# Attention's keys and first queries turned and split in the front's last units

## The chip, the cores and the metric

One core of one Trainium2 chip runs the whole kernel. The metric is device time in microseconds (us) of that core; a result is the median of several runs.

## What is computed

One layer of a hybrid backbone over 1024 latent tokens and 256 context tokens, width 1024, in fp32. What matters here is its first half:

```python
hc = _rms(ctx, norm1) * (1 + cc1) + ch1
kvc = hc @ w_in[:, OFF_K:OFF_G]                  # context keys and values
kc = _rms(kvc[..., :KV_W] per head, k_norm)
hx = _rms(x, norm1) * (1 + sc1) + sh1
zx = hx @ w_in                                   # 3 x 512 Hyena, 512 q, 128 k, 128 v, 2 x 1024 gates
q = _rope(_rms(q per head, q_norm), cos, sin)    # 8 heads of 64
k = _rope(_rms(k per head, k_norm), cos, sin)    # 2 heads of 64
y_b = _window_attention(q, k, v, kc, vc, sink)   # own block of 128 and its neighbours, all 256 context keys
```

`_window_attention` takes the softmax over the scores of at most 384 near keys (masked to a distance of 128), the 256 context keys and a sink logit. Then come the Hyena convolution, the merge of both branches, and 16 routed experts.

## The kernel before, in words

The kernel is a row of blocks, with a barrier of all engines between them: `front` (about 0 to 453 us), `attention` (to 619 us), then `spectra`, `convolve`, `merge`, `experts`. In each block every engine has its own instruction list, written out by hand, and semaphores order them. An engine runs its list in order: a wait holds all that stands behind it.

**Front.** Tokens are normed, modulated, turned and split into two parts, `h_hi` and `h_lo` (a rounded fp32r part and the rest), each 128 x 8 x 1280: eight slices of the width by 1280 token columns, the last 256 of them context. `w_in` is loaded in 17 units of 256 columns and split the same way by ScalarE (`high_part`) and VectorE (`weights_low`). TensorE (`project`, in the order of the list `groups`) makes each product of three fp32r matmuls (`three`, L220). Units 0 to 2 give q, k, v, written to `qkv` token by token; units 3 to 8 the Hyena inputs; units 9 to 16 the gates. `GATES` is 9, and from unit 3 on a unit is four groups (two halves of the columns by two halves of the tokens). ScalarE evicts each group from one of six banks. `first[u]` is the index of unit u's first group. A unit of gates is 96 matmuls of 512 columns on TensorE, some 22 us.

VectorE's list runs unit by unit, in this order: the low part of the next unit's weights; in units 9 and up, that unit's parts of the remaining modulation (`ada_part`, L620: two in each of units 9 to 11, one in unit 12, none later); then the norming and rotation of one token tile's heads (`norm_heads`, L647), from unit 4 to unit 13, ten tiles, the eight latent ones first and then the two of the context; in units 3 to 8 the short convolution. A part of the modulation waits for the load of its weights, which SyncE issues only when the part before is done (L389), and for the column sums that TensorE makes at the end of a unit (`column_sums`, L752) for the parts before it. VectorE signals each normed tile with the semaphore `qn_ready`. In unit 15 it makes the gate rows with a matmul of TensorE through the bank `p_rows` (L787).

**Attention** works in blocks of 128 queries (n = 0 to 7) by 8 heads, 64 steps u. Before the steps: TensorE turns the context's and the first two tiles' keys (`turn_k`, job NEAR) and the first queries (`turn_q`), ScalarE writes their high parts, VectorE their low parts and zeros, ScalarE copies the high part to the other half of the partitions (`k_beside`), four fills keep TensorE at work (`fill`, L1160: matmuls whose result nobody reads), and GpSimd makes three mask tables. Only then come the first scores (L1173). The keys of tiles 2 to 5 (MID) are handled at step 1, those of 6 and 7 (FAR) at step 3, and the next queries at step 4 of block 0 and step 1 of later blocks. A step is: scores of step u+2 (L1182 to L1189) once the exp of step u has freed their half of `p_s`; on VectorE the maximum and the shift of u+2 (L1071, L1073); exp on ScalarE (L1032); turning of the probabilities (L1197, L1203); their copies to `pT` by VectorE (L1083) and ScalarE (L1012). At steps 2 to 6 of a block the products with the values of the block before (L1223).

Keys stand in `kS` and `k_lo` (128 x 2 x 1280) with context first, so a block's near keys are one run of up to 384 columns.

Of the kernel before, what the change touches and what calls it, by code (L numbers as in the profile page):

```python
# [20 lines left out]
P = 128  # L21
D = 1024
L = 1024
# [110 lines left out]
def build(nc, A, out):  # L134
    root = ExitStack()
    with root:
# [37 lines left out]
        with ExitStack() as s12:  # L174
# [3 lines left out]
            with ExitStack() as s:  # L178
                sbh, _ = scope(s)

                with ExitStack() as below:
                    g["ada"] = scope(below)[0]("ada", [P, 2 * D // 512, KD, 512])
                g["h_hi"] = sbh("h_hi", [P, KD, LA], F32R)
                g["h_lo"] = sbh("h_lo", [P, KD, LA], F32R)
                front(g)
            g["tf"] = right.enter_context(nc.sbuf_tensor("dft_in", [P, 10, FC, LQ], F32, side="right"))
            g["decay"] = filters.enter_context(nc.sbuf_tensor("decay_in", [P, NT, HY], F32, side="right"))
            g["fpm"] = filters.enter_context(nc.sbuf_tensor("fpm", [H2, ORD, 2, HY], F32, side="right"))
            g["y_out"] = filters.enter_context(nc.sbuf_tensor("y_out", [P, 2, 512], F32, side="right"))
            g["y_stored"] = [nc.alloc_semaphore(name=f"y_stored{i}") for i in range(2)]  # L190
            attention(g)
# [35 lines left out]
def front(g):  # L227
# [30 lines left out]
    with ExitStack() as s:  # L258
# [7 lines left out]
        with ExitStack() as below:  # L266
# [3 lines left out]
            ub = sbb("ub", [P, L + 2])  # L270
# [4 lines left out]
            wrow = sbb("wrow", [P, NG, HD])  # L275
            cos, sin = sbb("cos", [P, NT, ROT]), sbb("sin", [P, NT, ROT])
            xn = sbb("xn", [P, NG, HD])
        x = sb("x_in", [P, NTA, D])
        hf = sb("hf", [P, 3, 512])
        rows1, rows2 = sb("rows1", [80, P]), sb("rows2", [56, P])  # L280
        junk = sb("junk", [P, D])[:]
# [40 lines left out]
        q_root, q_step, rope_step, qn_ready = sem("q_root_ready"), sem("q_step"), sem("rope_step"), sem("qn_ready")  # L322
        padded, conv_step, z_ready = sem("padded"), sem("conv_step"), sem("z_ready")
# [5 lines left out]
        ROWS_AT = UNITS - 2  # L329

# [5 lines left out]
        with nc.Block() as block:  # L336
            @block.sync
            def _(sp):
# [40 lines left out]
                sp.wait_ge(lo_ready, len(GROUPS))  # L379
                for u in range(UNITS):  # L380
                    if u == 2:
                        sp.wait_ge(sin_ready, 3)
# [23 lines left out]
            def _(pool):  # L406
# [6 lines left out]
                pool.memset(spare[0:H2, 6144:6144 + 2 * H2], 0.0).then_inc(f_zero, 1)  # L413

            @block.scalar
            def _(act):
# [19 lines left out]
                def evacuate(i):  # L436
# [10 lines left out]
                    else:  # L447
# [6 lines left out]
                        if h == 1:  # L454
                            act.wait_ge(evacuated, i + 1)
                            act.dma_start(g["gate_dram"][P * n:P * n + P, :], gs[:, n % 2, :])\
                               .then_inc(g_stored[n % 2], 16)

# [46 lines left out]
                act.wait_ge(padded, 1)  # L505
                for i in range(EARLY, len(groups)):
# [10 lines left out]
                    evacuate(i)  # L517

            @block.vector
            def _(dve):  # L520
# [126 lines left out]
                def norm_heads(i):  # L647


                    nonlocal rope_steps  # L650
                    x = qkv[:, i, 0:NG * HD].rearrange("p (h d) -> p h d", d=HD)
                    r_ = rstd[:, i, :].unsqueeze(2).broadcast_to([P, NG, HD])
                    if i:
                        dve.wait_ge(qn_ready, i)
# [14 lines left out]
                    dve.wait_ge(z_ready, min(2 * (i + 1), NZ))  # L669
# [33 lines left out]
                dve.memset(ub[:], 0.0).then_inc(padded, 1)  # L703
                dve.memset(ssq[:], 1.0).then_inc(ssq_ready, 1)
                dve.wait_ge(ssq_ready, 1)
                for u in range(UNITS):
# [7 lines left out]
                    if u == ROWS_AT:  # L714
                        gate_rows()
# [35 lines left out]
            def _(pe):  # L751
# [6 lines left out]

                def project(i):
# [19 lines left out]
                    if u >= 2 and i == last[u] - 1:  # L779
                        for m in (ada_parts(0) if u == 2 else []) + ada_parts(u - 1):  # L780
                            column_sums(m)
                    q = i - first[ROWS_AT] - 1
                    if 0 <= q < 4:
                        pe.wait_ge(diag_ready, q + 1)
                        if q:
# [80 lines left out]
def attention(g):  # L866
# [11 lines left out]
    with ExitStack() as s:  # L878
        sb, ps = g["scope"](s)
        nsink = sb("nsink", [P, NKV, GRP])  # L880
# [1571 lines left out]
```

## Time and profile before

| | us |
|---|---|
| median of 3 runs | 2245.38 |
| lowest, highest run | 2242.11, 2246.43 |
| span of the profiled execution | 2242.3 (its own time isn't listed) |
| front, start to last TensorE group | 452.4 |
| attention, to the first work of the next block | 453.8 to 619.7 |
| TensorE busy | 2145.9 |
| VectorE, ScalarE busy | 1655.7, 1147.0 |

A timeline row gives an instruction's start and duration, its engine (PE is TensorE, PEld its weight loads, DVE VectorE, ACT ScalarE, POOL GpSimd, SP SyncE), its line, what it writes and reads, and in brackets how long its engine was idle before it and who ended that. PEclk is TensorE's granted clock as a share of 2.4 GHz; it has two levels, 1.2 and 2.4 GHz, so a mean between 0.5 and 1 is a mix of both. A matmul's duration is longer than the spacing of a stream of them.

### The profile page before, as it was taken

How to read it: one execution, taken by the hardware profiler on the slowest of the kernel's cores; microseconds unless marked ns; L12 is line 12 of the kernel's file. 1: busy time of each engine (PE TensorE's matmuls, PEld its weight loads, DVE VectorE, ACT ScalarE, POOL GpSimd, SP SyncE). 2: the span in 40 equal slices, each digit the busy share in tenths (PEclk: the TensorE clock that was granted, in tenths of full speed). 3: DMA queues.
4: the chain of work that ended last, by engine and by line, in shares of the span. 5: the costliest groups of instructions: out<-in, count | busy, mean ns of one | idle time of the engine just before them, and what ended most of it. 6: DMA issues, size and time to landing. Idle time of an engine off the chain costs nothing.

```text
span 2242.3 us, 27253 instructions
## 1 busy us (share of the span) xinstructions
PE 2145.9 (96%) x10057; PEld 1695.6 (76%) x10057; DVE 1655.7 (74%) x1707; ACT 1147.0 (51%) x1201; POOL 175.8 (8%) x53
## 2 busy tenths in 40 slices
PE   7999999989999999999489999999999999999998
PEld 2998888856567776468468888888888888888886
DVE  3668754167654897553688889889889989898986
ACT  3521212165500220121257777777777777777775
POOL 0000000010000000000011011111011111011100
PEclk9999999999999999999789999999999999999999
DMA  8134454130020232643569999999999999999993
GB/s 305 61 98 163 142 178 141 47 118 13 17 80 6 70 131 91 221 168 113 197 236 364 393 394 380 380 378 380 399 391 380 378 382 384 396 387 380 380 378 121
DMA packets 183291, 539.38 MB, mean 241 GB/s; under 512 B 15231, under 2 KB 57355, under 8 KB 182708
## 3 DMA queue, kind: packets, MB, share of 16 engines
q1 hardware_dynamic: 172768, 506.72, 60.3%
q0 software_dynamic: 4752, 16.78, 2.9%
q10 hardware_dynamic: 5700, 14.90, 1.7%
q8 instruction: 48, 0.79, 0.1%
q14 instruction: 23, 0.19, 0.0%
HBM read 502.71 MB, written 35.65 MB: 240 GB/s over the span
## 4 chain that ended last, share of the span: by engine, by line
PE 49%; DVE 2%; DMA 0%; issue 0%; ACT 0%; POOL 0%; POOLq 0%
PE p_y L222 5%; PE p_y L224 5%; PE p_a L222 5%; PE p_a L224 5%; PE p_y L223 5%; PE p_a L223 5%; PE p_b L224 5%; PE p_b L223 5%; PE p_b L222 5%; PE p_t L2350 1%; PE p_t L2341 1%; DVE idx_rows L2305 1%; DVE late L2308 0%; DVE vals L2303 0%; DMA g1row<-xn_dram,idx_e 0%
## 5 line engine op out<-in xcount | busy, mean ns | idle before, releaser
L2246 DVE TENSOR_TENSOR r_lo<-ring,r_hi 128x2048 fp32r<-128x2048 f32 x384 | 865.8, 2287 | 62.8 <-ACT r_hi L2205 56.0
L2205 ACT ACTIVATE r_hi<-ring 128x2048 fp32r<-128x2048 f32 x384 | 731.0, 1915 | 154.4 <-PE p_b L224 74.7
L222 PE MATMUL p_y<-r_hi,a_hi 128*128 128x512 f32 x512 | 205.3, 401 | 0.0
L222 PE MATMUL p_a<-r_hi,x_hi 128*128 128x512 f32 x512 | 202.5, 396 | 1.0 <-DVE x_lo L2257 1.0
L224 PE MATMUL p_y<-r_hi,a_lo 128*128 128x512 f32 x512 | 200.0, 391 | 0.0
L224 PE MATMUL p_a<-r_hi,x_lo 128*128 128x512 f32 x512 | 199.8, 390 | 0.0
L223 PE MATMUL p_a<-r_lo,x_hi 128*128 128x512 f32 x512 | 199.2, 389 | 0.0
L223 PE MATMUL p_y<-r_lo,a_hi 128*128 128x512 f32 x512 | 199.2, 389 | 0.0
L222 PE MATMUL p_b<-r_hi,x_hi 128*128 128x512 f32 x512 | 199.2, 389 | 0.0
L223 PE MATMUL p_b<-r_lo,x_hi 128*128 128x512 f32 x512 | 199.2, 389 | 0.0
L224 PE MATMUL p_b<-r_hi,x_lo 128*128 128x512 f32 x512 | 199.2, 389 | 0.0
L222 PE MATMUL p_z<-h_hi,w_hi 128*128 128x512 f32 x448 | 177.0, 395 | 0.0
L224 PE MATMUL p_z<-h_hi,w_lo 128*128 128x512 f32 x448 | 174.5, 390 | 0.0
L223 PE MATMUL p_z<-h_lo,w_hi 128*128 128x512 f32 x448 | 174.4, 389 | 0.0
L2168 POOL DMA_INDIRECT g1row<-xn_dram,idx_e x16 | 121.4, 7587 | 58.5 <-issue 43.3
L2174 POOL DMA_INDIRECT out_x<-late,idx_s x17 | 45.3, 2666 | 914.6 <-DVE late L2296 914.6
L224 PEld LDWEIGHTS p_y<-r_hi,a_lo 128*128 128x128 f32 x512 | 96.1, 188 | 21.0
L224 PEld LDWEIGHTS p_a<-r_hi,x_lo 128*128 128x128 f32 x512 | 96.1, 188 | 20.5
L222 PEld LDWEIGHTS p_a<-r_hi,x_hi 128*128 128x128 f32 x512 | 96.2, 188 | 20.2 <-issue 1.4
L223 PEld LDWEIGHTS p_b<-r_lo,x_hi 128*128 128x128 f32 x512 | 96.1, 188 | 20.0
L222 PEld LDWEIGHTS p_b<-r_hi,x_hi 128*128 128x128 f32 x512 | 96.1, 188 | 20.0
L224 PEld LDWEIGHTS p_b<-r_hi,x_lo 128*128 128x128 f32 x512 | 96.1, 188 | 19.9
(319 smaller groups left out, 3577.7 us busy)
## 6 DMA issues: line engine op xcount, KB each, us to landing
ring<-in_w_gate SPq DMA_DIRECT2D x128, 1024.0 KB, 8.4
ring<-in_w_up SPq DMA_DIRECT2D x128, 1024.0 KB, 8.5
ring<-in_w_down SPq DMA_DIRECT2D x128, 1024.0 KB, 12.0
w_raw<-in_w_in SPq DMA_DIRECT2D x17, 1024.0 KB, 6.1
ada_rest<-in_ada_w SPq DMA_DIRECT2D x16, 1024.0 KB, 5.3
ada<-in_ada_w SPq DMA_DIRECT2D x8, 1024.0 KB, 15.3
gate_dram<-zs ACTq DMA_DIRECT2D x16, 512.0 KB, 2.6
x_normed<-gate_dram SPq DMA_DIRECT2D x16, 512.0 KB, 4.3
```

Of the source, the lines that this page charges most:

```text
L222: pe.matmul(out, a_hi, b_hi, start=start, stop=False)
L223: pe.matmul(out, a_hi, b_lo, start=False, stop=False)
L224: return pe.matmul(out, a_lo, b_hi, start=False, stop=stop)
L2168: pool.indirect_dma_start(out=xe[:], out_offset=None, in_=g["xn2_dram"][:, :], in_offset=bass.IndirectOffsetOnAxis(ap=idx_e[:, 0:1], axis=0))\
L2174: pool.indirect_dma_start(out=rows, in_=part, in_offset=None, out_offset=bass.IndirectOffsetOnAxis(ap=idx_s[:, at:at + 1], axis=0), comput ...
L2205: act.activation(r_hi[:, i % PARTS], ring[:, i % RAW], ACT.Copy).then_inc(hi_ready, 1)
L2246: dve.tensor_tensor(r_lo[:, i % PARTS], ring[:, i % RAW], r_hi[:, i % PARTS].bitcast(F32), ALU.subtract).then_inc(lo_ready, 1)
L2305: dve.max_index(rows[:, at], vals[:, at], aff).then_inc(found, 1)
L2341: mm = pe.transpose(p_t[:, bank, P * k:P * k + P], xe[:, P * (4 * q + k):P * (4 * q + k) + P], ident[:])
L2350: mm = pe.transpose(p_t[:, q % 2, P * k:P * k + P], au[:, q % 2, P * k:P * k + P], ident[:])
```

## The change

- The keys of all tiles and the queries of block 0 are turned and split in the front. TensorE does it through the bank `p_rows`, after the second group of unit 9 (NEAR), the second of unit 12 (MID), and the first (FAR) and third (queries) of unit 14. It waits for `qn_ready` of 4, 8, 10, 10. ScalarE and VectorE make the parts with the same instructions as before; the one new split is that NEAR's context and token parts go to two places, so its low part is four instructions of 256 columns.
- `norm_heads` takes the context tiles first (`HEAD_ORDER`), in units 4 and 5, and the latent tiles in units 6 to 13. So the eighth is tile 5, in unit 11.
- The latent keys' parts go into the columns of `h_hi` and `h_lo` that held the normed context tokens (columns 1024 to 1279 of each slice), 128 per key head: slice c holds the keys of tile c. A block's near keys are now up to three runs of 128 columns, 1280 columns apart. The context's keys have a buffer of their own.
- Queries of later blocks and probabilities take the places of the normed latent tokens.
- Masks and the sink table are made in the front; the front's buffers have other places, and the scratch `junk` lies in `ub`, of which now only the two edge columns are cleared.
- Attention begins with its scores. After the first two steps' scores come two fills (four before) and a wait for the table `sel`. The queries of block 1 are turned at step 1 of block 0.

The diff, cut to its core:

```diff
@@ front @@
+        HEAD_ORDER = list(range(NT, NTA)) + list(range(NT))
+        NEAR, MID, FAR, FIRST_Q = range(4)
+        KEY_TILES = ((NT, NT + 1, 0, 1), (2, 3, 4, 5), (6, 7))
+        TURNED_AT = {first[GATES] + 1: NEAR, first[GATES + 3] + 1: MID, first[GATES + 5]: FAR, first[GATES + 5] + 2: FIRST_Q}
+        NORMED = {NEAR: 4, MID: 8, FAR: NTA, FIRST_Q: NTA}
+        LOW_AT = {GATES + 1: (NEAR,), GATES + 4: (MID,), GATES + 5: (FAR, FIRST_Q)}
...
+            token = tile[rows, :, L + P * kv:L + P * kv + P]
+            beside = g["k_context"][rows, int(tile is h_lo), kv, :].rearrange("p (c t) -> p c t", t=P)
...
+                def turned_high(job):
+                    act.wait_ge(turned, job + 1)
...
+                    if job == NEAR:
+                        act.wait_ge(z_ready, NZ)
...
                     evacuate(i)
+                    if i in TURNED_AT:
+                        turned_high(TURNED_AT[i])
...
-                def norm_heads(i):
+                def norm_heads(p):
+                    i = HEAD_ORDER[p]
...
+                    if u == GATES:
+                        zero_beside()
...
                     if QKV_UNITS < u <= QKV_UNITS + NTA:
                         norm_heads(u - QKV_UNITS - 1)
+                    for job in LOW_AT.get(u, ()):
+                        turned_low(job)
...
+                def turn_early(job):
+                    pe.wait_ge(qn_ready, NORMED[job])
+                    if job == NEAR:
+                        pe.wait_ge(sin_ready, 3)
+                    else:
+                        pe.wait_ge(part_lo, job)
+                    if job == FIRST_Q:
+                        for j in range(GRP):
+                            mm = pe.transpose(p_rows[:, P * j:P * j + P], qkv[:, 0, P * j:P * j + P], ident[:])
+                    else:
+                        for n, t in enumerate(KEY_TILES[job]):
+                            mm = pe.transpose(p_rows[:, P * n:P * n + P], qkv[:, t, HD * NH:HD * NG], ident[:])
+                    mm.then_inc(turned, 1)
...
                             column_sums(m)
+                    if i in TURNED_AT:
+                        turn_early(TURNED_AT[i])
@@ attention @@
-                turn_k(K_NEAR, p_q)
-                turn_q(0, p_o)
-                fill(4)
-                pe.wait_ge(masks, 3)
-                pe.wait_ge(k_zero, NKV)
...
-                    pe.matmul(out[:, a:512], both, kS[:, kv, keys], start=True, stop=False)
-                    pe.matmul(out[:, a:512], both, k_lo[:, kv, keys], start=False, stop=False)
+                    pe.matmul(near, both, keys(h_hi, kv, n), start=True, stop=False)
+                    pe.matmul(near, both, keys(h_lo, kv, n), start=False, stop=False)
...
                 scores(0)
                 scores(1)
-                pe.wait_ge(qk_lo, 2)
-                turn_k(K_MID, p_q)
-                turn_k(K_FAR, p_o)
+                fill(2)
+                pe.wait_ge(small_in, 16)
...
-                    if h == turn_at(n) and n + 1 < NT:
-                        pe.wait_ge(qk_lo, q_job(n + 1) - 1)
+                    if h == 1 and n + 1 < NT:
+                        if n:
+                            pe.wait_ge(qk_lo, n)
```

## Rows read from the trace of the kernel before

**Rows 1.** The page, busy time of the engines: us, share of the span, instructions.
```profile
PE 2145.9 (96%) x10057; PEld 1695.6 (76%) x10057; DVE 1655.7 (74%) x1707; ACT 1147.0 (51%) x1201; POOL 175.8 (8%) x53
```

**Rows 2.** Table by stretches, 100 to 450 us: length, then engines' busy us.
```profile
sum 350.00, PE 350.00 PEld 295.65 DVE 191.00 ACT 67.18 POOL 0.00; mean PE 87.50 PEld 73.91 DVE 47.75 ACT 16.80 POOL 0.00
```

**Rows 3.** Timeline of attention, weight loads of four transposes: start, duration, instruction.
```profile
471.62 0.47 PEld L1152 LDWEIGHTS p_turned<-ident,qkv 128*128 128x128 f32 x4
```

**Rows 4.** Timeline, VectorE alone, gate units 10 and 11; in brackets idle before, releaser.
```profile
315.40 0.35 DVE L626 TENSOR_SCALAR ada_acc<-ada_rest,sil 128x256 f32<-128x256 f32 x1 [11.43 <-PE p_mod L755]
...
333.18 2.28 DVE L531 TENSOR_TENSOR w_lo<-w_raw,w_hi 128x2048 fp32r<-128x2048 f32 x1
338.08 0.35 DVE L626 TENSOR_SCALAR ada_acc<-ada_rest,sil 128x256 f32<-128x256 f32 x1 [2.61 <-PE p_mod L755]
...
347.37 0.35 DVE L626 TENSOR_SCALAR ada_acc<-ada_rest,sil 128x256 f32<-128x256 f32 x1 [5.29 <-DMA ada_rest<-in_ada_w]
...
355.21 0.49 DVE L678 TENSOR_TENSOR qkv<-work 128x320 f32<-128x320 f32 x1
```

**Rows 5.** Timeline, TensorE alone, end of unit 11 and unit 12.
```profile
337.46 0.95 PE L755 MATMUL p_mod<-ones,ada_acc 128*128 128x1 f32 x8
338.28 0.48 PE L222 MATMUL p_z<-h_hi,w_hi 128*128 128x512 f32 x1
...
349.26 0.39 PE L222 MATMUL p_z<-h_hi,w_hi 128*128 128x512 f32 x1
```

**Rows 6.** Timeline, all engines, from attention's start to its first scores.
```profile
453.81 1.81 DVE L1116 TENSOR_SCALAR k_lo<-ones 64x1280 fp32r<-64x1280 f32 x2 [17.09 <-PEq L336]
453.81 0.63 PE L1157 MATMUL p_turned<-ident,qkv 128*128 128x128 f32 x4 [1.45 <-PEq L336]
...
454.71 3.60 PE L1163 MATMUL p_context<-qkv,ident 128*128 128x512 f32 x8
...
458.07 1.28 ACT L1032 ACT_TABLE_LOAD   x1
...
458.77 0.35 PE L1182 MATMUL p_s<-kS,qS 128*128 128x256 f32 x1 [0.46 <-DVE qS L1054]
```

**Rows 7.** Timeline, all engines, attention's first block of queries.
```profile
461.52 0.39 PE L1182 MATMUL p_s<-kS,qS 128*128 128x256 f32 x1 [0.66 <-ACT probs L1032]
...
463.15 1.18 ACT L992 ACTIVATE kS<-p_turned 64x512 fp32r<-64x512 f32 x2
...
465.65 0.69 ACT L1032 ACTIVATE probs<-p_s,nm 128x512 f32<-128x512 f32 x1
...
466.49 0.39 PE L1182 MATMUL p_s<-kS,qS 128*128 128x256 f32 x1 [2.01 <-ACT probs L1032]
...
469.76 0.69 ACT L1032 ACTIVATE probs<-p_s,nm 128x512 f32<-128x512 f32 x1
...
474.27 1.39 DVE L1054 TENSOR_TENSOR qS<-p_turned,qS 64x512 fp32r<-64x512 f32 x2
...
475.72 0.60 PE L1182 MATMUL p_s<-kS,qS 128*128 128x384 f32 x1 [2.18 <-DVE qS L1054]
```

**Rows 8.** TensorE's timeline at 51 us; then stretches: us, busy, granted clock, DMA.
```profile
51.06 0.35 PE L222 MATMUL p_z<-w_hi,h_hi 128*128 128x256 f32 x1 [3.09 <-DVE w_lo L531]
...
52.00:56.00 4.00, 4.00 (x24) 4.00 (x23) 3.90 (x7) 1.83 (x4) 0.00 (x0) 0.57 0.87 263
...
476.00:480.00 4.00, 3.99 (x21) 3.14 (x20) 1.86 (x5) 1.37 (x4) 0.00 (x0) 0.59 0.00 0
...
728.00:735.00 7.00, 6.31 (x20) 4.88 (x21) 0.00 (x0) 2.04 (x4) 0.00 (x0) 0.53 0.97 309
```

**Rows 9.** Groups by line and form, 450 to 620 us: busy us, mean ns.
```profile
L1182 PE MATMUL p_s<-kS,qS 128*128 128x384 f32 x48 | 21.4, 445 | 2.4 <-DVE qS L1054 2.2 <-ACT probs L1032 0.3
...
L1152 PEld LDWEIGHTS p_turned<-ident,qkv 128*128 128x128 f32 x28 | 3.3, 141 | 0.0
```

**Rows 10.** One line's instructions, L1544: ns least, median, most; first and last start.
```profile
L1544 PEld LDWEIGHTS p_j<-ident,ya x64: 195/212/231, 726.4 to 831.2; 128*128 128x128 f32 x64
```

More of the change, by code:

```diff
@@ L188, in build @@
[L188 to L191, printed above, removed]
+                g["masks"] = [sbh(n, [P, P], BF16) for n in ("negI", "m_prev", "m_next")]
+                g["nsink"], g["sinks"] = sbh("nsink", [P, NKV, GRP]), sbh("sinks", [P, GRP, NKV])
@@ new lines, in build @@
+                with ExitStack() as below:
+                    sbw, _ = scope(below)
+                    g["wrow"] = sbw("wrow", [P, NG, HD])
+                    g["cos"], g["sin"] = sbw("cos", [P, NT, ROT]), sbw("sin", [P, NT, ROT])
+                    g["xn"] = sbw("xn", [P, NG, HD])
+                sbh("head_space", [P, 1792])
+                front(g)
+                g["tf"] = right.enter_context(nc.sbuf_tensor("dft_in", [P, 10, FC, LQ], F32, side="right"))
+                g["decay"] = filters.enter_context(nc.sbuf_tensor("decay_in", [P, NT, HY], F32, side="right"))
@@ L192, in build @@
+                g["fpm"] = filters.enter_context(nc.sbuf_tensor("fpm", [H2, ORD, 2, HY], F32, side="right"))
+                g["y_out"] = filters.enter_context(nc.sbuf_tensor("y_out", [P, 2, 512], F32, side="right"))
+                g["y_stored"] = [nc.alloc_semaphore(name=f"y_stored{i}") for i in range(2)]
+                attention(g)
             give_back()
@@ L889, in attention @@
         r_t = sb("r_t", [NH, 2, P])
-        probs = sb("probs", [P, 3, 640])
-        pT = sb("pT", [P, 2, NKV, 5, GRP, P])
+        probs = parts[:, 1, KD - 3:KD, 0:640]
+        pT = [[parts[:, b, 0:5, 512 * kv:512 * kv + 512].rearrange("p c (j t) -> p c j t", j=GRP) for kv in range(NKV)]
+              for b in range(2)]
         o_raw = sb("o_raw", [P, 512])
@@ L918, in rows, with keys, context @@
             return slice(HD * kv, HD * kv + HD)
-        NEAR_JOB, MID_JOB, FAR_JOB = 1, 3, 4
-        KEYS = {NEAR_JOB: (0, 512), MID_JOB: (512, 1024), FAR_JOB: (1024, LA)}
-        KEYS_AT = {1: MID_JOB, 3: FAR_JOB}
+        def keys(table, kv, n):
+            b = blocks(n)
+            return table[:, b[0]:b[-1] + 1, L + P * kv:L + P * kv + P]
+        def context(side, kv):
+            return g["k_context"][:, side, kv, :]
         def values_bank(n):
             return p_w if n == NT - 1 else p_o
-        def turn_at(n):
-            return 1 if n else 4
-        def q_job(n):
-            return n + 4 if n else 2
         with nc.Block() as block:
@@ L1130, in _ @@
                     window_copy(u)
[L1131 to L1133 removed]
+                    if h == 2 and n + 1 < NT:
                         q_low(n + 1, p_q)
@@ L1153, in turn_q @@
                     mm.then_inc(qk_turned, 1)
-                def turn_k(tiles, bank):
-                    for i, t in enumerate(tiles):
-                        mm = pe.transpose(bank[:, P * i:P * i + P], qkv[:, t, HD * NH:HD * NG], ident[:])
-                    mm.then_inc(qk_turned, 1)
                 def fill(count):
@@ L1187, in scores @@
                         pe.matmul(out[:, 512 - P:512], negI[:], m_next[:], start=False, stop=True)
-                    pe.matmul(out[:, 512:768], both, kS[:, kv, 0:LC], start=True, stop=False)
-                    pe.matmul(out[:, 512:768], both, k_lo[:, kv, 0:LC], start=False, stop=True).then_inc(s_done, 1)
+                    pe.matmul(out[:, 512:768], both, context(0, kv), start=True, stop=False)
+                    pe.matmul(out[:, 512:768], both, context(1, kv), start=False, stop=True).then_inc(s_done, 1)
                 def turn_probs(u):
```

213 lines of the change are left out of this document (118 added, 95 removed).

## The prediction

> **What bounds the kernel now.** I read three things in turn. The page first: TensorE is busy for 96% of the span, and the places where it isn't are few [rows 1]. Then a table by stretches over the front: from 100 to 450 us TensorE is busy in every microsecond, VectorE in 191 of the 350 and ScalarE in 67 [rows 2]. So in the front each microsecond in which TensorE waits, or transposes, is a microsecond of the kernel. Then the timelines, at the two places that the change touches: gate units 11 and 12 of the front, and the first 25 us of attention. Barriers stand between front, attention and what follows, and nothing that the change touches crosses them but loads that land long before their use, so a shift at either place reaches the end whole.
>
> **The front: what is added.** Fourteen transposes move into TensorE's stream: 4 for the near keys, 4, 2 and 4. Four of them take 0.47 us of weight loads, which set their pace, in attention [rows 3]: 14 x 0.118 = 1.6 us, and with an estimated 0.1 us for each of four switches 2.0 us. I find no cover: 1.6 to 2.4.
>
> **The front: a new wait.** The middle keys are turned after the second group of unit 12, and TensorE waits there until eight tiles are normed. The new order puts the context tiles first, so tile 5 is the eighth, at the place where tile 7 stands now: VectorE's work of unit 11, behind that unit's two parts of the modulation. That place is tied to TensorE and to a load: part 13 waits for the column sums at the end of TensorE's unit 11 (337.46) and starts at 338.08; part 14 waits 5.29 us for its load, which is issued only when part 13 is done; the norming follows, and its last write ends at 355.21 + 0.49 = 355.70 [rows 4, 5]. TensorE starts unit 12 at 338.28 and is through its second group at 349.26, where the third group's first matmul starts now [rows 5]. It would wait 355.70 - 349.26 = 6.4 us. Behind it stand all further projections; VectorE's next parts and ScalarE's evictions wait for TensorE and move with it, so nothing makes up for it. Whether VectorE can be there sooner or later: the moved zeroing (1.81 us [rows 6], unit 9) and the near keys' low part (four halves of 256 columns, estimated at 1.7 us from 1.39 for two of 512 [rows 7], unit 10) lie ahead of it. The zeroing goes into a wait of 11.43 us at 315.40; the low part delays the low weights of unit 12 from 333.18 + 2.28 to 337.2, with TensorE wanting them at 338.28, so it costs nothing, with about 1 us to spare [rows 4]. The other three turnings have their tiles and parts in time: the near ones need the fourth norming, from unit 7; the last tile is normed in unit 13, with one part of the modulation in unit 12 and none in 13, some 10 us before unit 14's first group ends.
>
> A wait of this length lowers the clock behind it. After 3.09 us without TensorE work the clock is at its lower level, 1.2 GHz, for most of 52 to 56 us (mean 0.57); later in the kernel it stays there from 728 to 735 us (0.53) [rows 8]. In a stream without gaps I take the first, 3.4 us at half speed: 1.7 us, with 0 and 3.5 as ends. The Trainium skill (TensorE: Matmul & The Clock Gate, HAM oscillation) says that a long wait between matmul bursts makes the next burst start slow; by that rule too the wait costs more than its length, and the trace agrees.
>
> Small things. The masks go to the front's start, where GpSimd has nothing else; they were ready ahead of the queries' low part, so nothing is gained by it. On SyncE one small load goes ahead of the norm weights, and VectorE waits for it before the low weights of unit 2, where it has time. The padding's clearing shrinks, and only ScalarE waited for it. In all these the cover is TensorE's unbroken stream [rows 2], so 0 for each; if the small load came late, VectorE's slack there would have to be used up first. **Front: 2.0 + 6.4 + 1.7 = 10.1 us more** (8.0 to 12.3).
>
> **Attention's start: what goes.** Now the first scores start at 458.77, after the keys and queries were turned, copied and split, and the third scores at 461.52 [rows 6, 7]. Changed, TensorE starts scores as its first work at 453.81: 4.96 us sooner. Then two fills stand in its queue, of 0.9 us each (eight matmuls in 3.60) [rows 6]: 1.2 + 1.8 = 3.0 us from first to third scores, where they are now 2.75 apart. So the third scores come 4.7 us sooner. The new wait there for the selection table costs nothing if its load (issued at about 453.8) lands by 456.8; the trace shows only that two such loads had landed before the scores at 458.77, so up to 1.9 us could be lost. VectorE and ScalarE have nothing ahead of the first maximum and the first exp; the activation table load of 1.28 us, now at 458.07 [rows 6], then starts at 453.8 and ends before the first exp at about 455.7. The Trainium skill (ScalarE: Activation LUTs, What ACT_TABLE_LOAD costs) adds a drain of 1.38 us to each load; by that figure the estimate is an exp 0.8 us later, and the third scores about 0.5 us later. No row here separates a drain from idle time, and the sum leaves it out.
>
> **The first block of queries.** From the third to the ninth scores it now takes 461.52 to 475.72 = 14.2 us [rows 7]. In it ScalarE splits the middle keys (463.15 to 465.65), so that the third exp, whose bank the fifth scores wait for, starts at 465.65 instead of about 463.4: the fifth scores come at 466.49 instead of 464.3, 2.2 us. The far keys hold the fifth exp until 469.76 and cost 1.1 us in the same way. The next queries are turned at the block's fifth unit, and their low part (474.27 + 1.39) holds the ninth scores until 475.72 instead of about 473.4: 2.3 us [rows 7]. These 5.6 us go. In return the next queries are turned at the second unit: 1.2 us of ScalarE and 1.39 of VectorE, half of what the middle keys took of ScalarE; I take half their loss, 1.1 (0.4 to 2.2). Gain 4.5 us (3.0 to 5.2). With it goes the idleness ahead of 475.72, behind which the clock is 0.59 for 4 us [rows 8]: up to 1.7 us, I take 1.2, for TensorE still waits a little here. Later blocks issue the same instructions on other addresses. **Attention: 4.7 + 4.5 + 1.2 = 10.4 us less** (11.6 = 4.7 + 5.2 + 1.7; at the least 5.8, with the load's 1.9 lost, 3.0 for the block and nothing for the clock).
>
> **The sum** is -0.3 us. The three runs shown have a median of 2245.38; the profiled execution's span is 2242.3, near the lowest of them (2242.11), and its own time isn't listed. On the median: 2245.1. I call changes within 0.2% (4.5 us, about what can be told from none) no change; this comes out so because the new wait pays back what attention's start gains.
>
> **Rivals.**
> A: the wait in unit 12 doesn't come, because the eighth norming is done earlier than I read. For it: VectorE is idle for nearly half of these units [rows 2]. Against: the idleness is waiting for TensorE and a load [rows 4]. Then front +2.0, attention -10.4: 2237.0, faster. 0.15.
> B: it is slower, by the keys' new layout. The near keys are read in up to three runs of 128 columns, 1280 apart, by 128 matmuls. The first of each 384-column pair takes 445 ns as a contiguous read [rows 9]; no row shows such a read. The nearest are transposes of every fourth element, whose weight loads take 212 ns [rows 10] against 141 for contiguous ones [rows 9], though that is a step at each element and here it is one in 128. At 71 ns each: 9.1 us, and with the forecast's -0.3 2254.2. It decides from 35 ns each (4.5 us). 0.06.
> C: the wait comes and the low clock behind it lasts 7 us, as at 728, while the first block keeps part of its losses and its low clock: front 12.3, attention 7.5: 2250.2. 0.12.
> D: the wait comes without a low clock and attention gives its most: 8.4 - 11.6: 2242.2. 0.17.
> Forecast: 0.5.
>
> **Numbers.** 2245.1, range 2237 to 2251: from A to C, which leaves B and the far ends out. Faster by over 0.2% is A with some of D's tail: 0.19. Slower is B and the half of C and its tail: 0.15. Within: 0.66.
>
> **What would show it.** TensorE idle for about 6 us behind the second group of unit 12, ended by VectorE's last rotation write, then 3 to 4 us of matmuls at 1.2 GHz; four short bursts of transposes; the front's last matmul some 10 us later; first scores right at attention's start, third scores 3.0 us behind; ninth about 13 behind the first; no clock below 1 at the second block. I am wrong if the transposes of the middle keys follow their group without a gap, or if near-key matmuls are longer than before.

## The result, and the profile after

| | before | changed |
|---|---|---|
| median of 5 runs, us | 2245.45 | 2253.72 |
| lowest, highest | 2242.11, 2246.86 | 2252.21, 2255.94 |
| span of the profiled execution | 2242.3 | 2251.7 |

The ratio is 1.0039, with a 95% interval of 1.0026 to 1.0051: slower by 8.3 us, outside the predicted range of 2237 to 2251.

Both halves of the prediction, front and attention, can be looked up. The new wait comes first, in the timeline of TensorE alone, units 11 and 12, changed kernel (start, duration, instruction, idle before it and who ended it):

```profile
344.14 0.95 PE L873 MATMUL p_mod<-ones,ada_acc 128*128 128x1 f32 x8
...
362.81 1.11 PE L888 MATMUL p_rows<-ident,qkv 128*128 128x128 f32 x4 [6.37 <-DVE qkv L761]
363.58 0.77 PE L241 MATMUL p_z<-h_hi,w_hi 128*128 128x512 f32 x1
...
365.44 0.50 PE L242 MATMUL p_z<-h_lo,w_hi 128*128 128x512 f32 x1
365.77 0.39 PE L243 MATMUL p_z<-h_hi,w_lo 128*128 128x512 f32 x1
```

And VectorE alone, which ends it:

```profile
339.97 0.42 DVE L797 TENSOR_TENSOR h_lo<-p_rows,h_hi 64x256 fp32r<-64x256 f32 x1
340.42 2.29 DVE L613 TENSOR_TENSOR w_lo<-w_raw,w_hi 128x2048 fp32r<-128x2048 f32 x1
344.75 0.35 DVE L708 TENSOR_SCALAR ada_acc<-ada_rest,sil 128x256 f32<-128x256 f32 x1 [2.04 <-PE p_mod L873]
...
354.44 0.35 DVE L708 TENSOR_SCALAR ada_acc<-ada_rest,sil 128x256 f32<-128x256 f32 x1 [5.69 <-DMA ada_rest<-in_ada_w]
...
362.27 0.48 DVE L761 TENSOR_TENSOR qkv<-work 128x320 f32<-128x320 f32 x1
362.68 2.28 DVE L613 TENSOR_TENSOR w_lo<-w_raw,w_hi 128x2048 fp32r<-128x2048 f32 x1
```

These rows answer to [rows 4, 5]: VectorE does the same work in the same order, with the near keys' low part (`h_lo`, 339.97) put ahead of it. The wait was forecast at 6.4 us and is 6.37. The clock behind it, in the table by stretches (length, busy us of PE, PEld, DVE, ACT, POOL with counts, granted clock, DMA):

```profile
356.00:360.00 4.00, 0.44 (x2) 0.00 (x1) 3.82 (x8) 0.60 (x1) 0.00 (x0) 0.85 0.49 162
360.00:362.80 2.80, 0.00 (x0) 0.00 (x0) 2.73 (x8) 0.00 (x0) 0.00 (x0) 0.50 0.99 340
362.80:364.00 1.20, 1.19 (x5) 1.19 (x6) 1.20 (x1) 0.03 (x1) 0.00 (x0) 0.50 0.10 32
364.00:366.00 2.00, 2.00 (x6) 1.53 (x6) 0.96 (x1) 1.94 (x4) 0.00 (x0) 0.59 0.00 0
366.00:368.00 2.00, 2.00 (x10) 1.63 (x9) 0.00 (x0) 0.47 (x1) 0.00 (x0) 1.00 0.92 235
```

TensorE is granted 1.2 GHz from about 358.8, inside the wait, until about 365.6 (0.59 over the two us from 364). What lies between 362.81 and 365.77, four transposes and five matmuls of 512 columns, takes 2.96 us; at the full clock it would be 0.47 + 5 x 0.234 = 1.64 (0.234 is the spacing of this kernel's stream at the full clock). So the low clock costs 1.3 us by this sum (forecast 1.7), and 1.4 by run 4 below.

Attention, TensorE alone, again the changed kernel:

```profile
470.95 0.40 PE L243 MATMUL p_z<-h_hi,w_lo 128*128 128x512 f32 x1
472.83 0.36 PE L1242 MATMUL p_s<-h_hi,q_first 128*128 128x256 f32 x1 [1.48 <-PEq L374]
...
475.61 0.49 PE L1242 MATMUL p_s<-h_hi,q_first 128*128 128x256 f32 x1
...
485.74 0.41 PE L1242 MATMUL p_s<-h_hi 128*128 128x384 f32 x1
...
489.34 0.45 PE L1242 MATMUL p_s<-h_hi 128*128 128x384 f32 x1 [0.37 <-ACT h_parts L1126]
```

These rows answer to [rows 6, 7]. The third scores come 2.78 us behind attention's start (7.71 before, so 4.93 sooner; forecast 4.7), the ninth 10.13 us behind the third (14.20 before; 4.07 gained, forecast 4.5). Attention now ends 156.4 us after its first scores at 472.83 (next block's first matmul at 629.26, L1408), where it took 619.76 - 453.81 = 165.95: **9.5 us less**, against 10.4 forecast.

But the front's last matmul starts at 470.95, and before it was at 451.97: **19.0 us later**, not 10.1. That is the miss, and the page of the profile shows where to look. Section 5 of the changed kernel's page has the same matmul form in the experts (`p_b`) and in the front (`p_z`); the mean ns of one is the last number before the second bar:

```profile
L241 PE MATMUL p_b<-r_hi,x_hi 128*128 128x512 f32 x512 | 199.2, 389 | 0.0
...
L241 PE MATMUL p_z<-h_hi,w_hi 128*128 128x512 f32 x448 | 181.0, 404 | 0.0
L243 PE MATMUL p_z<-h_hi,w_lo 128*128 128x512 f32 x448 | 177.8, 397 | 0.0
L242 PE MATMUL p_z<-h_lo,w_hi 128*128 128x512 f32 x448 | 177.8, 397 | 0.0
```

And the same group in the kernel before, its page:

```profile
L222 PE MATMUL p_z<-h_hi,w_hi 128*128 128x512 f32 x448 | 177.0, 395 | 0.0
L224 PE MATMUL p_z<-h_hi,w_lo 128*128 128x512 f32 x448 | 174.5, 390 | 0.0
L223 PE MATMUL p_z<-h_lo,w_hi 128*128 128x512 f32 x448 | 174.4, 389 | 0.0
```

The front's projections of units 3 to 16, whose instructions the change leaves alone, are longer by 7 to 9 ns each, from the first one of unit 3 on. The starts say it more sharply. Take the time from one matmul's start to the start of the third after it, a sum of three spacings: it is 680 ns before, in every unit, and 702 to 703 now. 1344 matmuls / 3 x 21.5 ns = 9.6 us. That is an estimate from spacings; runs 4 and 10 below, which differ in the weights' place alone, put their last projection at 463.16 and 454.00 and so make it 9.2 us. With the wait 6.4, the clock 1.4 and the transposes 2.0 (run 10) that is the whole of the 19.0.

No wait explains it: the idle column says 0.0. What the change did do to this stream is in the layout. In units 3 to 16 the weights are the loaded (stationary) operand and the tokens the moving one. `h_hi` and `h_lo` stand where they stood, at bytes 57472 and 98432 of each partition. The four weight tiles stood at byte 157824 and, one behind the other, 8192 further each; in the changed kernel `w_hi0` begins at 169952. The slices that the matmuls take out of these tiles start multiples of 256 bytes into them, so a tile's start modulo 256 holds for every slice.

### The profile page after: what moved, and what is told of

Read it like the earlier page. It is cut to its first block, busy times and chain, and to the rows that moved or that the text cites. A ratio compares the mean times of both kernels' runs of the same rounds, so it can differ in the third digit from the quotient of the medians.

```text
span 2251.7 us, 27262 instructions
## 1 busy us (share of the span) xinstructions
PE 2152.8 (96%) x10053; PEld 1695.6 (75%) x10053; DVE 1654.9 (73%) x1712; ACT 1147.9 (51%) x1205; POOL 174.8 (8%) x53
## 4 chain that ended last, share of the span: by engine, by line
PE 49%; DVE 2%; DMA 0%; issue 0%; ACT 0%; POOL 0%; POOLq 0%
PE p_y L241 5%; PE p_a L241 5%; PE p_y L243 5%; PE p_a L243 5%; PE p_y L242 5%; PE p_a L242 5%; PE p_b L241 5%; PE p_b L242 5%; PE p_b L243 5%; PE p_t L2406 1%; PE p_t L2397 1%; DVE idx_rows L2361 1%; DVE late L2364 0%; DVE vals L2359 0%; DMA g1row<-xn_dram,idx_e 0%
## 6 DMA issues: line engine op xcount, KB each, us to landing
ada<-in_ada_w SPq DMA_DIRECT2D x8, 1024.0 KB, 15.3
```

## The experiments

"Tokens" are `h_hi` and `h_lo`, "weights" the four tiles `w_hi0`, `w_lo0`, `w_hi1`, `w_lo1`; numbers 0 and 1 serve even and odd units. "Three spacings" is the sum above, the median of the 84 such sums inside the four groups of a unit, worked out from the starts in the trace. A ratio is to the kernel before, run beside it.

**1. Weights moved in the kernel before** (`e1`).

```diff
-        w_hi, w_lo = [sb("w_hi0", [P, KD, UW], F32R)], [sb("w_lo0", [P, KD, UW], F32R)]
+        def shifted(t, at):
+            return t[:, at:at + KD * UW].rearrange("p (k n) -> p k n", k=KD)
+        AT = (8, 8, 8, 8)
+        w_hi = [shifted(sb("w_hi0", [P, KD * UW + 16], F32R), AT[0])]
+        w_lo = [shifted(sb("w_lo0", [P, KD * UW + 16], F32R), AT[1])]
...
```

> The kernel before, with one thing changed: each of the four tiles of split weights is 64 bytes longer and its weights start 32 bytes into it, so that they start at an address that is 32 modulo 64, as in the changed kernel, instead of 0 modulo 64. Nothing of the change itself is in it. Theory (place of the stationary operand): the front's matmuls of 512 columns, whose stationary operand is a weight tile, follow each other at 0.234 us instead of 0.227, a group of 24 takes 5.62 instead of 5.44 us, and the 56 such groups of units 3 to 16 bring about 10 us: about 2255, 1.0045 of before. Rival 1 (the spacing comes from what VectorE, ScalarE or the loads do at the same time in the changed kernel, in their new places or order): spacing stays 0.227 and the time 2245. Rival 2 (the moving operand, the tokens, which did not move, must lie at a certain distance from the weights): some other spacing, the same in even and odd units only by chance.

Measured: 2249.47 (10 runs), ratio 1.0023 (1.0013 to 1.0032), three spacings 693 in odd units, 695 to 696 in even ones, and 700 in unit 3, although it has the same tiles as the other odd units. So moving the weights alone, in a kernel without the change, slows the stream: rival 1 falls. But 693 isn't 703, and the time rose by half of what was expected: the start modulo 64 isn't the whole of it.

**2. Weights moved back in the changed kernel** (`e2`).

```diff
-        ss, rt, r0, tt = (sb(n, [P, NTA]) for n in ("ss", "rt", "r0", "tt"))
+        stats = sb("stats", [P, 4, NTA])
+        ss, rt, r0, tt = (stats[:, i] for i in range(4))
```

> The changed kernel, with the four small tiles of the tokens' norm (40 bytes each, padded to 64) made one tile of 160 bytes, so that everything behind it, the weights too, lies 96 bytes lower: the four weight tiles start at 0 modulo 64 instead of 32. Theory (place of the stationary operand): spacing back to 0.227 us, a group back to 5.44, 10 us less than the changed kernel's 2253.7: 2243.5, about 0.999 of before; the wait in unit 12 stays and is about 6.4 us. Rival 1 (other engines' traffic): spacing 0.234 and 2253.7, 1.004 of before. Rival (VectorE sets the wait in unit 12 and not the stream): with the faster stream the wait grows by what unit 12's first groups gain, below 0.5 us.

Measured: 2244.51, ratio 1.0001 (0.9991 to 1.0011); three spacings 680 in every unit; the wait in unit 12 is still 6.4 us. Saving 96 bytes of scratch, with nothing else changed, takes off 8.5 us (0.0038 of the time).

**3. Mixed places** (`e3`: offsets of 4, 0, 0 and 8 elements in place of the four 8).

> The kernel before with its weight tiles lengthened as in the first of these runs, but started at different places: the high weights of even units 16 bytes past a multiple of 64, the low weights of even units at 0, the high weights of odd units at 0, the low weights of odd units at 32. Of three matmuls two load high weights and one loads low weights. Theory, with each load costing by its own start: in odd units a third of the loads is out of place and a group takes 5.44 + 8 x 0.007 = 5.50 us. In even units two thirds are, at 16 bytes: 5.56 if any start off 64 costs the same, 5.44 if only the 32nd byte matters, more than 5.56 if 16 bytes are worse. Rival (it is the pair of tiles, high against low or weights against tokens, that has to match): even and odd units do not follow these counts.

Measured: 2249.28 (one run); 694 in even units, 697 in odd ones. Neither count of the theory fits: in odd units two of three loads stand at 0 modulo 64, as before, and yet these units are no faster than the even ones. The rule of 64 bytes falls.

**4. The middle keys turned later in the changed kernel** (`e4`).

```diff
-        TURNED_AT = {first[GATES] + 1: NEAR, first[GATES + 3] + 1: MID, ...
+        TURNED_AT = {first[GATES] + 1: NEAR, first[GATES + 4] + 1: MID, ...
```

> The changed kernel, with the middle keys turned after the second group of unit 13 instead of unit 12; the weights stay at 32 modulo 64. By then all ten tiles are normed. Theory: the 6.4 us of waiting in unit 12 go and with them the stretch at the lower clock behind it, about 1.5 us: 8 us less than the changed kernel, 2245.8, ratio to before 1.000. Rival (VectorE is short of time there and the wait moves to the far keys or the first queries in unit 14, where TensorE waits for the middle keys' low part): less than 3 us gained, 2251 or more, with a new gap behind the first or third group of unit 14.

Measured: 2244.97, ratio 1.0002 (0.9992 to 1.0011); 702 to 703 still, and the transposes follow their group without a gap:

```profile
379.76 0.60 PE L888 MATMUL p_rows<-ident,qkv 128*128 128x128 f32 x4
```

So the wait and the low clock behind it were worth 8.3 us (1.0039 - 1.0002 of the time). The starts of the last projection, 470.95 in the changed kernel and 463.16 here, give 7.8: the wait of 6.4 and 1.4 for the clock. The profiled execution has, besides, no low clock around 730 us, where run 2's has one (last section); nothing shows that this edit did that.

**5 and 6. One place for each unit** (`s1`, `s2`). One kernel holds many experiments if the offset is chosen by unit. The edit of the first of the two:

```diff
+        OFF = ((0, 0, 0, 0, 8, 16, 24, 8, 0, 4, 0, 16, 1, 24, 0, 8, 12),
+               (0, 0, 0, 0, 8, 16, 24, 0, 8, 4, 0, 0, 1, 0, 24, 24, 12))
+
+        def shifted(tiles, lo, u):
+            at = OFF[lo][u]
+            return tiles[u % 2][:, at:at + KD * UW].rearrange("p (k n) -> p k n", k=KD)
...
```

> The kernel before, its four weight tiles lengthened by 128 bytes, and the weights of each unit started at another place in them. Bytes past a multiple of 128 for (high, low), units 3 to 16: (0,0) (32,32) (64,64) (96,96) (32,0) (0,32) (16,16) (0,0) (64,0) (4,4) (96,0) (0,96) (32,96) (48,48). The spacing of the matmuls of a unit is read from the trace. Theory 1 (the start modulo 64 of the loaded weights decides, the lot of high and low together): 227 ns in units 3, 5, 10, 11 and about 234 where both are off, between them where one is off. Theory 2 (modulo 128): 227 in units 3 and 10 alone. Theory 3 (nothing local: the whole layout or the program decides, since the two earlier runs with moved weights both gave 232 however their starts differed): all units alike, at 227 or at 232.

> As the run by units before it, and the low part of the tokens, the moving operand of every third matmul, starts 32 bytes past a multiple of 128 instead of 0. Theory A (only the loaded weights' place matters): the same spacing unit by unit as in that run. Theory B (the moving operand's start costs as well): 227 nowhere, and the matmuls that read the low tokens are spaced wider by themselves. Theory C (what counts is whether the operands start at the same place within 64 or 128 bytes): the unit with both weight parts 32 bytes off becomes one of the faster.

Measured: 2248.49 and 2251.39 (one run each). In the first, three spacings in units 3 to 16 are 693 699 696 700 693 700 707 693 693 700 695 693 694 691. No theory fits: units 3 and 10 too, which were meant to stand as before, have 693. The rows of unit 10 say which matmul it is (groups by form):

```profile
L223 PE MATMUL p_z<-h_lo,w_hi 128*128 128x512 f32 x24 | 9.5, 396 | 0.0
L222 PE MATMUL p_z<-h_hi,w_hi 128*128 128x512 f32 x24 | 9.3, 389 | 0.0
L224 PE MATMUL p_z<-h_hi,w_lo 128*128 128x512 f32 x23 | 9.1, 397 | 0.0
```

High weights with high tokens (389) are as before; the two beside them, with the low tokens (396) and with the low weights (397), aren't. And since each tile had been made 128 bytes longer, the low weights stood at another place modulo 256 than the high ones. The second run was spoilt in a like way: the padding beside the low tokens had moved the weights by 128 bytes too, no unit had all operands alike (its sums are 693 to 700), and it can't say what a moving operand out of place costs by itself.

Modulo 256 everything so far falls into line. Tokens and weights both start at 128 in the kernel before and in run 2 (680). In the changed kernel weights start at 224 and tokens at 128 (703). In the kernel before, the experts' loaded and moving tiles all start at 192 (680), while the output projection loads tokens that start at 224 and streams weights that start at 64 (700). That was noticed after six runs; the runs that follow put it to the test.

**7. High and low together, by unit** (`s3`; both in one tile, 8192 bytes apart).

> The kernel before; high and low weights of a unit now lie in one tile, 8192 bytes apart, and each unit starts both by the same distance past the place of the first units. Distances in bytes, units 3 to 16: 0 0 256 96 32 64 128 16 160 192 224 4 128 96. Where the distance is 0 or 256, weights and tokens start at the same place modulo 256. Theory (the loaded weights and the moving tokens must start at the same place modulo 256; it fits all runs so far, and the output projection and the experts of the kernel before too: 233 ns where they differ, 227 where they are alike): three spacings together are 680 ns in units 3, 4 and 5 alone, and 690 to 707 in the others; 703 in units 6 and 16, which stand as in the changed kernel. Rival (modulo 128): 680 in units 9 and 15 as well. Rival (modulo 64): also in units 8 and 12.

| bytes past the tokens' place modulo 256 | 0 | 0 | 256 | 96 | 32 | 64 | 128 | 16 | 160 | 192 | 224 | 4 | 128 | 96 |
|---|---|---|---|---|---|---|---|---|---|---|---|---|---|---|
| unit | 3 | 4 | 5 | 6 | 7 | 8 | 9 | 10 | 11 | 12 | 13 | 14 | 15 | 16 |
| three spacings, ns | 680 | 680 | 680 | 703 | 701 | 702 | 695 | 700 | 700 | 687 | 700 | 696 | 696 | 702 |

Measured: 2249.75 (one run). Out of place, the single sums often alternate between two values (698 and 702 in unit 8, 690 and 704 in unit 9, whose mean is 697), so a difference of a few ns between two such units means little; the 680 have no such spread. Units 4, 6 and 9 in the groups by form:

```profile
L222 PE MATMUL p_z<-h_hi,w_hi_lo 128*128 128x512 f32 x16 | 6.2, 389 | 0.0
L223 PE MATMUL p_z<-h_lo,w_hi_lo 128*128 128x512 f32 x15 | 5.8, 389 | 0.0
...
L222 PE MATMUL p_z<-h_hi,w_hi_lo 128*128 128x512 f32 x18 | 7.1, 396 | 0.0
L223 PE MATMUL p_z<-h_lo,w_hi_lo 128*128 128x512 f32 x18 | 7.1, 396 | 0.0
...
L223 PE MATMUL p_z<-h_lo,w_hi_lo 128*128 128x512 f32 x23 | 9.1, 394 | 0.0
L222 PE MATMUL p_z<-h_hi,w_hi_lo 128*128 128x512 f32 x22 | 8.8, 398 | 0.0
```

The theory's forecast holds in every unit but one (12, with 687 instead of at least 690). In particular 128 bytes apart is slow and 256 is fast: it is modulo 256.

**8. High or low alone** (`s4`).

> The same, but with distances of their own for the high and the low weights: (0,0) (0,32) (32,256) (0,128) (128,256) (128,128) (0,64) (64,256) (256,256) (0,256) (96,256) (0,96) (160,256) (0,160), units 3 to 16; 256 counts as 0. Theory of the run before it, with each load judged by itself: 680 ns for three matmuls in units 3, 11 and 12; where the low weights alone are off (units 4, 6, 9, 14, 16) one load in three is late, where the high ones alone are (5, 7, 10, 13, 15) two are, so the latter lose about twice as much. Rival (one operand out of place moves all three, since the stream keeps a fixed rhythm): about 693 in all of them, as units 3, 10 and 14 of the first run by units suggest.

| high, low | 0,0 | 0,32 | 32,0 | 0,128 | 128,0 | 128,128 | 0,64 | 64,0 | 0,0 | 0,0 | 96,0 | 0,96 | 160,0 | 0,160 |
|---|---|---|---|---|---|---|---|---|---|---|---|---|---|---|
| unit | 3 | 4 | 5 | 6 | 7 | 8 | 9 | 10 | 11 | 12 | 13 | 14 | 15 | 16 |
| three spacings, ns | 680 | 700 | 694 | 693 | 700 | 695 | 693 | 700 | 680 | 680 | 689 | 699 | 694 | 700 |

Measured: 2253.67 (one run). It is 680 in units 3, 11 and 12 and nowhere else. With the low weights alone out of place, one load in three, three spacings are 13 to 20 ns longer; with the high ones alone, two in three, 9 to 20; with both by 128 bytes, 15. So a load isn't priced by itself, as the theory had it. The rival is nearer, though its "about 693" is 689 to 700.

**9. Everything moved, and the output projection** (`s6`, on the kernel before).

```diff
         right, filters = ExitStack(), ExitStack()
+        root.enter_context(nc.sbuf_tensor("above_hid", [P, 40], F32, side="right"))
...
+                sbh("ahead_of_the_front", [P, 8])
                 with ExitStack() as below:
                     g["ada"] = scope(below)[0]("ada", [P, 2 * D // 512, KD, 512])
```

> The kernel before with the whole front moved up by 32 bytes (tokens and weights, both at 160 modulo 256 then, 32 modulo 64), and 160 bytes put above the tiles on the right side, so that the output projection's turned tokens, which it loads, start at 64 modulo 256 like the output weights, which move, instead of at 224. Theory (only the difference counts): the front stays at 227 ns per matmul, and the projection's 384 matmuls go from 233.3 to 227, 2.5 us less in all: 2243, ratio 0.999. Rival (the absolute place counts, 32 modulo 64 being slow): the front goes to about 234, 10 us more. Rival for the projection (its spacing comes from its pauses): 233 stays, ratio 1.000.

Measured: 2240.39, ratio 0.9982 (0.9973 to 0.9992). The front keeps 680 in every unit with all operands at 160 modulo 256, which is 32 modulo 64: the common place is free, the difference counts. The output projection goes from 700 to 680 (groups by form, before and in this run):

```profile
L222 PE MATMUL p_m<-wo_hi,mT_hi 128*128 128x512 f32 x128 | 52.3, 408 | 0.0
L223 PE MATMUL p_m<-wo_lo,mT_hi 128*128 128x512 f32 x128 | 51.2, 400 | 0.0
L224 PE MATMUL p_m<-wo_hi,mT_lo 128*128 128x512 f32 x128 | 50.8, 397 | 0.0
```

```profile
L224 PE MATMUL p_m<-wo_hi,mT_hi 128*128 128x512 f32 x128 | 50.9, 397 | 0.0
L226 PE MATMUL p_m<-wo_hi,mT_lo 128*128 128x512 f32 x128 | 49.9, 390 | 0.0
L225 PE MATMUL p_m<-wo_lo,mT_hi 128*128 128x512 f32 x128 | 49.9, 390 | 0.0
```

From its first to its last matmul the projection takes 105.9 us where it took 109.7: 3.8 us, of which the spacings are 2.6. The rest goes with the clock (table by stretches within the projection, before and in this run):

```profile
1014.00:1020.00 6.00, 6.00 (x27) 5.10 (x27) 2.18 (x10) 2.00 (x5) 0.00 (x0) 0.72 0.48 124
...
1012.00:1020.00 8.00, 8.00 (x53) 7.19 (x53) 4.07 (x13) 2.73 (x7) 0.00 (x0) 1.00 0.36 108
```

**10. The changed kernel with both mended** (`e5`: edits 2 and 4).

> The changed kernel with both edits that each took off what the result showed in excess: the small tiles merged, so that the weights start at 0 modulo 128, and the middle keys turned in unit 13. Theory: the two gains are apart, 9.3 and 8.3 us, so 2253.7 - 17.6 = 2236, ratio to before 0.9961, faster by attention's 9.5 us less the transposes. Rival (they overlap, since the wait in unit 12 takes up what the slower stream would cost in VectorE's shadow): 2240 or more.

Measured: 2235.96, ratio 0.9971 (0.9960 to 0.9982): faster than both kernels. The two edits add up within the intervals: 1.0039 - 0.9971 is 15.3 us, and by themselves they took 8.5 and 8.3. (The forecast's ratio, 0.9961, lies at the interval's edge; that its 2236 was met to the decimal is luck.) By its page the stream is back, and the timeline shows attention's first scores:

```profile
L241 PE MATMUL p_z<-h_hi,w_hi 128*128 128x512 f32 x448 | 177.7, 397 | 0.0
L243 PE MATMUL p_z<-h_hi,w_lo 128*128 128x512 f32 x448 | 174.6, 390 | 0.0
L242 PE MATMUL p_z<-h_lo,w_hi 128*128 128x512 f32 x448 | 174.4, 389 | 0.0
```

```profile
454.00 0.39 PE L243 MATMUL p_z<-h_hi,w_lo 128*128 128x512 f32 x1
455.88 0.36 PE L1243 MATMUL p_s<-h_hi,q_first 128*128 128x256 f32 x1 [1.48 <-PEq L375]
```

The front's last matmul starts 454.00 - 451.97 = 2.03 us later than before: the price of the 14 transposes and their switches alone, forecast 2.0.

**11. The second block's queries late again** (`e9`, on run 10).

```diff
-                    if h == 1 and n + 1 < NT:
+                    if h == (1 if n else 4) and n + 1 < NT:
...
```

ScalarE's and VectorE's parts of these queries move from `h == 2` to `h == 5` in the same way.

> The changed kernel with the weights at the tokens' place modulo 256 and the middle keys turned in unit 13, and, as in the kernel before, the second block's queries turned at the fifth unit of the first block instead of the second. The prediction's term: their low part again holds the ninth scores, 2.3 us, and ScalarE's early copy no longer delays the first block's exps, 1.1 us back: from third to ninth scores 10.15 + 1.2 = about 11.3 us, and up to 1.7 us of low clock behind the wait come on top: 2237 to 2239 where the same kernel without this edit had 2236.0. Rival (the early copy costs nothing, so that its whole 2.3 us of gain is lost): third to ninth 12.5 us, 2238.3 to 2240. Rival (the low part hides behind other waits): no difference.

TensorE's timeline, first, third, ninth, tenth and eleventh scores:

```profile
456.02 0.36 PE L1243 MATMUL p_s<-h_hi,q_first 128*128 128x256 f32 x1 [1.48 <-PEq L375]
...
458.80 0.50 PE L1243 MATMUL p_s<-h_hi,q_first 128*128 128x256 f32 x1
...
469.79 0.69 PE L1243 MATMUL p_s<-h_hi 128*128 128x384 f32 x1 [2.35 <-DVE h_hi L1146]
...
472.07 0.67 PE L1243 MATMUL p_s<-h_hi 128*128 128x384 f32 x1
...
474.15 0.45 PE L1243 MATMUL p_s<-h_hi 128*128 128x384 f32 x1 [0.26 <-ACT h_parts L1127]
```

Third to ninth takes 10.99 us where run 10 has 10.15 and before it was 14.20: the early turning is worth 0.84 us (forecast 1.2), and the rest of the block's gain, 3.2 of 4.05, comes from the keys. The wait for the low part is back (2.35), the clock behind it is 0.72 over 468 to 474 us, and the ninth to the eleventh scores take 4.36 us where run 10 has 3.59: 0.8 us of clock. Together 1.6 us at this place. The totals, 2238.55 (ratio 0.9972, 0.9961 to 0.9983) and 2235.96 (0.9971), were taken at different times, and their intervals can't tell 1.6 us apart.

**12. With the output projection's tiles alike too** (`e8`, run 10 and `sbuf_tensor("above_late", [P, 40], F32, side="right")` ahead of `late`).

> The changed kernel with the weights at the tokens' place modulo 256, the middle keys turned in unit 13, and 160 bytes above the tiles that follow attention on the right side, so that the output projection's turned tokens and its weights start alike modulo 256 too. Theory (loaded and moving operand alike modulo 256): the projection's 384 matmuls of 512 columns go from 233 to 227 ns, 2.5 us less than the same kernel without the last edit (2236.0 in its session): 2233.5, ratio to before about 0.9960. Rival (the projection hides it behind VectorE or ScalarE): 2236, 0.9971.

Measured: 2230.75, ratio 0.9942 (0.9928 to 0.9955), the fastest of all. By the spans, 2228.8 against 2232.6 in run 10, it is 3.8 us, more than the 2.5 forecast, and all of it lies in the projection (109.7 and 105.9 us from first to last matmul). What isn't spacing is clock (table by stretches, run 10 and then this one):

```profile
1004.00:1010.00 6.00, 6.00 (x29) 5.14 (x29) 2.34 (x11) 2.01 (x5) 0.00 (x0) 0.72 0.40 105
```

```profile
1004.00:1010.00 6.00, 6.00 (x33) 5.12 (x33) 2.18 (x10) 1.50 (x5) 0.00 (x0) 1.00 0.57 182
```

A stretch at the lower level within the projection, worth up to 0.28 x 6 = 1.7 us (1.3 by what the spacings leave), doesn't come. It is hardly chance: all twelve traces whose projection runs at 700 have this stretch, and the two at 680, runs 9 and 12, don't. How the spacing, or the place of the tiles, keeps it away is open.

## Why the prediction was wrong

- **Transposes, 2.0 us:** right (2.03, run 10, all that the changed front still costs there).
- **The wait in unit 12, 6.4 us:** right to 0.03 us, with what holds it: the column sums, then a load that is issued late, then the norming. Rival A falls. Run 4 shows that the place of the turning alone makes it.
- **The low clock behind it, 1.7 us:** came, 1.3 to 1.4 us. The low stretch is 6.8 us long, but 4.0 of it lie inside the wait; so rivals C (7 us behind the wait) and D (none) fall. The Trainium skill's rule (TensorE: Matmul & The Clock Gate, HAM oscillation) held here in kind.
- **Attention's start, 4.7 us:** it gave 4.9. The selection table cost nothing: no wait shows ahead of the third scores. The first exp starts at 474.69, 0.62 us after the table load's end at 474.07 and as soon as its shift is there, so there is no room for the drain of 1.38 us that the Trainium skill (ScalarE: Activation LUTs, What ACT_TABLE_LOAD costs) adds to a load; behind the load it would have put the exp at 475.45.
- **The first block, 4.5 us:** it gave 4.1, within its bounds (whose low end, by its own terms, is 5.6 - 2.2 = 3.4 and not 3.0). The late turning of queries was put at a net 1.2 us and is 0.84.
- **The low clock at the second block, 1.2 us:** it goes as forecast, but was mis-sized. Run 11, where that wait is put back, gives 0.8; and of attention's 9.5 us only 9.5 - 4.9 - 4.1 = 0.5 are left for it and all else.
- **Rival B, the strided keys:** falls. The near keys' matmuls of 384 columns take 437 ns in the mean as the first of a pair, though they read up to three runs 1280 columns apart. The 445 of [rows 9] is no larger in truth: two of its 48 fell in the low clock (603 and 668 ns), and the median is 442.
- **The step that failed:** the front's sum, 2.0 + 6.4 + 1.7 = 10.1, has no term for the projections themselves. The change puts the front's buffers in other places, and the prediction costed that at nothing without a reason; it took an address to have no price (of the later blocks it even says "the same instructions on other addresses"). In fact the weights moved from the tokens' place modulo 256 to 96 bytes beside it, and 1344 matmuls follow each other some 7 ns later each: 9.2 us between runs 4 and 10. By the spans the changed kernel is 9.4 us longer where 0.3 less was forecast. Of this miss of 9.7 us the stream is 9.2; the front's other terms came out 0.3 better (19.0 - 9.2 = 9.8 against 10.1), which is the clock, and attention's 0.9 worse.

The kernel before could have said so: its experts' matmuls have means of 389 to 401 ns on its page and its output projection's 397 to 408, the same instruction form. The means overlap, for they take in starts of groups and the low clock; three spacings, 680 against 700, don't. Such a difference between equal forms was there to be asked about.

## What to carry to other kernels

When a change moves buffers, compare the spacing of one and the same matmul form across all stages and both kernels, and list the start of each loaded and each moving operand modulo 256 bytes; a few bytes of padding or a few small tiles made one may be worth more than the change itself. A turning that waits for the last link of a chain on another engine belongs one unit later, if its result has time. Offsets chosen by loop step turn one run into a dozen measurements.

## What was not expected of the hardware

- In this kernel a stream of fp32r matmuls of 512 columns with a weight load of 128 columns each runs at 226.7 ns if loaded and moving operands start at the same place modulo 256 bytes (0 bytes apart or 256), whatever that place is (128, 160, 192 and 64 tried), and at 229 to 236 if not; the worst had the high weights 16 and the low ones 144 bytes apart from the tokens (707 ns for three), the mildest both 192 (687). Why it is 256, and what collides, is open; single operands out of place slow their neighbours too. Out of place the offsets don't fix the price: run 1 has 700 in unit 3 and 693 in the other odd units with the same tiles. A moving operand out of place by itself, other formats and other widths were not tried.
- Whether a short low stretch of the clock comes at a given pause changes from one trace to the next without any edit near it. Around 722 to 734 us of run 2 and, at the same work, 716 to 727 us of run 10:

```profile
726.00:734.00 8.00, 5.81 (x23) 4.71 (x24) 0.70 (x1) 2.28 (x4) 0.00 (x0) 0.71 0.63 198
```

```profile
719.00:727.00 8.00, 6.43 (x34) 5.62 (x35) 0.08 (x1) 3.00 (x6) 0.00 (x0) 1.00 0.73 222
```

  That is up to 0.29 x 8 = 2.3 us of clock that differ at a place which no edit touches. Each trace is one execution, and executions of one kernel differ in this too: 25 of the kernel before have spans from 2238.7 us (mean granted clock 0.984) to 2245.8 (0.979). So a change of a few us is better read in its own stretch than in the total.
